# Router in the output projection, a first gather for one pair, and the last pair's down projection by column halves

## The chip, the cores and the metric

One core of one Trainium2 chip runs the whole program in one launch. The metric is the device time of an execution in microseconds. The median of three runs of the kernel before is 4315.71 us (4311.06 to 4321.27).

## What is computed

Two transformer blocks over 512 latent tokens (and 256 context tokens) of width 1024 in float32, and a third one at whose end stands a mixture of experts. Only the end of that third block is touched: the output projection `w_o` with its residual and norm, and the mixture, in which each expert picks its own 64 tokens of the 512:

```
x_mid = x + mod_x[2] * (merged @ w_o)
h2 = modulate(rms(x_mid, norm2_g), mod_x[3], mod_x[4])
affinity = softmax(h2 @ router_w)                     # 512 x 16 experts
gate, idx = top_k(affinity.T, 64)                     # 64 tokens for each expert
xe = h2[idx]                                          # 16 x 64 x 1024
hid = silu(xe @ w_gate[e]) * (xe @ w_up[e])           # 1024 x 1408 each
ye = (hid @ w_down[e]) * gate                         # 1408 x 1024
out = x_mid + mod_x[5] * scatter_add(ye, idx)
```

The three weight tensors of the 16 experts are 277 MB, and each is read once.

## The kernel before, in words

A kernel is a row of phases. Each ends with a clearing of its semaphores by SP and a barrier of all engines (`phase`). Within a phase each engine runs its own instruction list and waits on semaphores; all loads and stores are issued by SP, in program order, on one hardware queue.

**Output projection** (`closing`, tag `wo`). 512 tokens are four tiles of 128. For each of two column blocks and four tiles, eight matmuls accumulate (L488), PSUM bank `u % 6`. Behind the last block's tiles VectorE forms `x`, ScalarE its sum of squares, VectorE the normed tile `y` (`x_hat`, L579). TensorE turns it, two tiles behind (`behind = 2`, `turn`, L451, eight transposes into banks 6 and 7), and ScalarE and VectorE take four blocks each with the modulation (L516, L586) into `hT`. SP loads the router's weights once block 0 is done (`then`, L72).

**Router** (`route`). SP loads three constants (L4357 to L4359), and then the nine first ring pieces. TensorE makes the logits, four tiles x eight matmuls with 16 columns (L4369). VectorE and ScalarE make the softmax (L4403 to L4408). TensorE turns the affinities to 16 rows of 512, VectorE finds the 64 largest of each row in eight rounds of `max` and `match_replace`, TensorE turns the mask back and ranks it, and `picks` (L4434) writes the one-hot matrix `pick` (token x slot) for the first four experts, 256 slots.

**Experts** (`experts`). SP first loads three vectors (`experts_cols`, L4480 to L4482) and the last gate (L4483, 512 KB). TensorE gathers the first four experts' tokens: for each of eight blocks of features k, four matmuls over the token tiles (`gather`, L4501), stationary `x_hat[:, tile, k::8]`, moving `pick` with 256 columns. A float32 matmul is two weight loads and two matmul instructions in the trace, a transpose one of each. ScalarE applies the modulation (`take`, L4619), which needs `mul` (L4638), made from the three vectors; TensorE's first expert matmul waits for all eight blocks. VectorE picks for the other 12 experts once the gate has landed.

The experts go in eight pairs. The two of a pair have 64 slots each and stand side by side in the array's columns. For each step j of eight, 12 matmuls (24 instructions, L4572) use the step's two pieces (gate and up rows j of either expert, 2 x 1408 floats of each partition, 1.44 MB) and accumulate in six banks; side 0 and side 1 write different banks at a time (`(m % 2) ^ side`). Then `hid` is formed, turned (L4586), and the down projection (L4605) goes over 11 row blocks of 128 in pieces of two rows (1.05 MB), into banks 6 and 7, again crosswise. VectorE multiplies by the gate (L4688), and eight matmuls of the scatter (L4514) bring the result back to tokens, with an addition each (L4648). Between the steps stand `fillers`, in a fixed order: in pair 0 four blocks of the next gather and then eight turns of the gated picks (L4509), two fillers after each of the first steps (`max(10 - 2 * j, 0)`); in later pairs gathers for pairs ahead and the scatter of the pair before. After the last pair come its gating, eight scatters, eight additions and four stores of 512 KB (L4494).

The ring has room for nine gate-and-up pieces. `expert_places` lays 224 pieces into it; a piece that would run over the end starts at 0. Each piece waits in SP for the release of the last piece that lay in its place. Pieces 0 to 8 wait for nothing. Piece 9 waits for piece 0, and so on to 16 (the first down piece) for 7; 17 waits for 8, 18 for 9, and from there several small ones go into the place of one large one. A step's two pieces are released by its last matmuls, before the fillers behind it.

## Time and profile before

| what | us |
|---|---|
| median of the runs | 4315.71 |
| the profiled execution's own time | 4313.52 |
| its span | 4311.7 |
| output projection ends, route starts | 3599.1, 3599.9 |
| experts phase starts | 3635.2 |
| first expert matmul | 3654.0 |
| last down matmul ends | 4298.7 |

Over the span TensorE is busy 92%, VectorE 37%, ScalarE 20%, GpSimd 16%. The table of slices shows the last 16% of the span with DMA at 400 to 422 GB/s and TensorE at 8 to 9 tenths; in the two slices before, DMA moves 40 and 145 GB/s. The share of busy time is a mean over stages of different kinds, so it must be read together with the slices: in one stage the matmuls may set the pace, in another the loads.

### The profile page before, as it was taken

Reading aid. Unit: us, or ns where it says so; the run is one execution under the profiler, and the core shown is the slowest. Engines: PE = TensorE matmul, PEld = TensorE weight load, DVE = VectorE, ACT = ScalarE, POOL = GpSimd, SP = SyncE. Lnnn points to the kernel's source line nnn. Section 1 sums busy time; section 2 is a strip of 40 time slices with the busy share of each in tenths; the row PEclk is TensorE's granted clock in tenths of the full one; section 3 lists DMA queues with packets and bytes.
Section 4 is the critical chain, followed back from the end, with each engine's and each line's share of the span. In section 5 each row is a group of like instructions: output and inputs, shape, how many; then the busy total and the mean of one; then the engine's idle time right before and its main releaser. Section 6 shows DMA issues by size and latency. Waiting matters only on the chain. (4 is left out here: it accounts for less than half of the span.)

```text
span 4311.7 us, 50124 instructions
## 1 busy us (share of the span) xinstructions
PE 3985.8 (92%) x20395; PEld 2380.8 (55%) x20395; DVE 1590.6 (37%) x2962; ACT 850.7 (20%) x1656; POOL 690.9 (16%) x513
## 2 busy tenths in 40 slices
PE   7997889999989999899988999989998897999988
PEld 4665445554446766588546666664554445433433
DVE  2346442224734464433464454530123323111111
ACT  3224320000123332200013233320123201000000
POOL 0003212223411111122333232310002200000000
PEclk9998999999999999999998999999999997999999
DMA  4117511113431111353341010104200313999998
GB/s 171 40 37 256 191 40 59 59 59 132 167 98 44 40 45 59 111 207 133 128 122 46 23 28 21 37 21 150 62 1 1 156 40 145 401 421 422 422 421 368
DMA packets 317260, 580.04 MB, mean 135 GB/s; under 512 B 55933, under 2 KB 186333, under 8 KB 316393
## 3 DMA queue, kind: packets, MB, share of 16 engines
q1 hardware_dynamic: 317032, 576.84, 36.4%
q8 instruction: 164, 2.69, 0.2%
q14 instruction: 64, 0.52, 0.0%
HBM read 566.15 MB, written 10.63 MB: 134 GB/s over the span
## 5 line engine op out<-in xcount | busy, mean ns | idle before, releaser
L3018 PE MATMUL dn_ps<-room,dn_w 128*128 128x512 f32 (+1 forms) x616 | 229.7, 526 | 5.2 <-DVE dn_qx L3556 3.5
L776 PE MATMUL ffn_up_ps<-room,ffn_up_w 128*128 128x384 f32 (+1 forms) x704 | 209.0, 441 | 12.4 <-DMA ffn_up_w<-in_ffn_w_gate 12.4
L776 PE MATMUL ffn_up_ps<-ffn_up_t,room 128*128 128x384 f32 (+1 forms) x704 | 205.9, 436 | 1.0 <-DVE room L856 1.0
L776 PE MATMUL ffn_up_ps<-room 128*128 128x384 f32 (+1 forms) x704 | 203.9, 432 | 0.0
L4572 PE MATMUL experts_ps<-experts_ring,experts_xs 128*64 128x512 f32 (+1 forms) x768 | 165.5, 582 | 28.0 <-DMA experts_ring<-in_w_up 28.0
L776 PEld LDWEIGHTS ffn_up_ps<-room,ffn_up_w 128*128 128x128 f32 x704 | 135.3, 194 | 71.6 <-DMA ffn_up_w<-in_ffn_w_gate 13.2
L4572 PE MATMUL experts_ps<-experts_ring,room 128*64 128x512 f32 (+1 forms) x768 | 162.7, 576 | 8.0 <-DMA experts_ring<-in_w_up 7.3
L3018 PEld LDWEIGHTS dn_ps<-room,dn_w 128*128 128x128 f32 x616 | 117.0, 195 | 96.0 <-issue 82.5
L2415 PE MATMUL hgrn_ps<-room,hgrn_w 128*128 128x512 f32 x372 | 168.7, 593 | 0.7 <-DMA hgrn_w<-in_odd_w_in 0.7
L776 PEld LDWEIGHTS ffn_up_ps<-ffn_up_t,room 128*128 128x128 f32 x704 | 134.7, 192 | 58.1 <-DVE room L856 2.3
L1051 PE MATMUL ffn_down_ps<-ffn_down_w_sums,ffn_down_hid_sums 128*128 128x512 f32 x330 | 163.2, 604 | 2.2 <-DVE ffn_down_w_sums L1139 2.2
L776 PEld LDWEIGHTS ffn_up_ps<-room 128*128 128x128 f32 x704 | 133.8, 190 | 55.7
L4605 PE MATMUL experts_ps<-experts_ring,experts_hidT 128*64 128x512 f32 x704 | 154.6, 594 | 10.5 <-issue 5.6
L4648 DVE TENSOR_TENSOR x_sb<-x_sb,experts_ps 128x512 f32<-128x512 f32 x64 | 44.0, 687 | 302.9 <-PE experts_ps L4514 302.9
L863 DVE TENSOR_TENSOR room<-ffn_up_ps,room 128x384 f32<-128x384 f32 (+1 forms) x154 | 73.3, 488 | 222.2 <-PE ffn_up_ps L776 222.2
L2412 PE MATMUL hgrn_ps<-hgrn_w,room 128*128 128x384 f32 (+1 forms) x480 | 144.0, 451 | 0.0
L4572 PEld LDWEIGHTS experts_ps<-experts_ring,experts_xs 128*64 128x64 f32 x768 | 59.4, 141 | 135.1 <-issue 132.1
L488 PE MATMUL out_ps<-out_w,room 128*128 128x512 f32 x296 | 130.4, 599 | 0.8 <-ACT room L530 0.8
L1051 PE MATMUL ffn_down_ps<-ffn_down_w,ffn_hid 128*128 128x512 f32 x220 | 116.5, 612 | 15.3 <-DMA ffn_down_w<-in_ffn_w_down 14.5
L834 POOL TENSOR_TENSOR room<-ffn_up_w 128x512 f32<-128x512 f32 x44 | 56.7, 1289 | 439.6 <-PE ffn_up_ps L776 233.0
L188 PE MATMUL in_ps<-in_w,room 128*128 128x512 f32 (+1 forms) x296 | 119.9, 565 | 0.6 <-DMA in_w<-in_w_in 0.6
L1139 DVE TENSOR_TENSOR ffn_down_w_sums<-ffn_down_w,ffn_down_w_sums 128x512 f32<-128x512 f32 x55 | 81.9, 1490 | 96.9 <-POOL ffn_down_w_sums L1114 96.9
(628 smaller groups left out, 6891.9 us busy)
## 6 DMA issues: line engine op xcount, KB each, us to landing
experts_ring<-in_w_gate SPq DMA_DIRECT2D x128, 704.0 KB, 15.5
experts_ring<-in_w_up SPq DMA_DIRECT2D x128, 704.0 KB, 17.8
experts_ring<-in_w_down SPq DMA_DIRECT2D x160, 512.0 KB, 14.3
ffn_down_w<-in_ffn_w_down SPq DMA_DIRECT2D x55, 1024.0 KB, 4.9
att_wm<-in_mod_w SPq DMA_DIRECT2D x20, 2048.0 KB, 9.2
ffn_up_wm<-in_ada_w SPq DMA_DIRECT2D x12, 2048.0 KB, 12.5
ffn_up_w<-in_ffn_w_up SPq DMA_DIRECT2D x22, 1024.0 KB, 7.7
ffn_up_w<-in_ffn_w_gate SPq DMA_DIRECT2D x20, 1024.0 KB, 5.5
```

Of the source, the lines that this page charges most:

```text
L188: mm = nc.tensor.matmul(ps[:, u % 8, 0:wd], xT[:, k, t * P:(t + 1) * P], ahead.tile[:, k, 0:wd] if j == 0 and k < n_ahead else wt[:, j % r ...
L488: mm = nc.tensor.matmul(ps[:, u % BANKS, 0:wd], xT[:, k, t * P:(t + 1) * P], wt[:, j % ring, k, 0:wd], start=k == 0, stop=k == kt - 1)
L776: mm = nc.tensor.matmul(result(n, p), lhs[:, k, :], rhs[:, k, :], start=k == 0, stop=k == half - 1)
L834: nc.gpsimd.tensor_tensor(s[:, 0, :, :], quarter(n, 1, lo), quarter(n, 1, hi), ALU.add).then_inc(S["s1_done"], 1)
L863: nc.vector.tensor_tensor(kept(n, to), result(n, p), kept(n, q), ALU.add).then_inc(done, 1)
L1051: mm = nc.tensor.matmul(result(p, prod), lhs, rhs, start=j == 0, stop=j == STEPS - 1)
L1139: nc.vector.tensor_tensor(t[:, 1, :], hi[:, right], t[:, 0, :], ALU.subtract).then_inc(S["t2_done"], 1)
L2412: mm = nc.tensor.matmul(ps[:, bank, 0:b - a], hT[:, k, t * P:(t + 1) * P], wt[:, s, k, 0:b - a], start=k == 0, stop=k == KD - 1)
L2415: mm = nc.tensor.matmul(ps[:, bank, :], weights(j, k)[:, piece * P:(piece + 1) * P], hT[:, k, CTX:], start=k == 0, stop=k == KD - 1)
L3018: mm = nc.tensor.matmul(out, ahead.tile[:, k, :] if k < by_ahead else wt[:, h % 2, piece, k, :], hT[:, k, tok], start=k == 0, stop=k == KD ...
L4572: mm = nc.tensor.matmul(ps[out_rows, 3 * n + c, 0:b - a], xs_now[:, j, at:at + SLOTS], ring[:, w_at + a:w_at + b], start=j == 0, stop=j == ...
L4605: mm = nc.tensor.matmul(ps[out_rows, 6 + half, :], hidT[:, f, out_rows], ring[:, w_at:w_at + 512], start=f == 0, stop=f == FT - 1)
```

## The change

The `Router` object holds the router's weights, the constants (identity, upper triangle, ones, slot numbers) and room for the softmax. Its five loads are issued where that of the router's weights was. The logits of a tile are made in `closing`, one turn behind, in bank 2. The exponentials and the reciprocal of their sum are made at the end of the same phase. `route` begins with their product. The first picks are for two experts, 128 slots, and the first gather as well; the other half of that group of four experts ("second") is eight fillers ahead of the others in pair 0, which are now up to three after a step. The picks in `experts` are for 14 experts. The last pair's down projection goes over all 11 row blocks for columns 0 to 511, and then for columns 512 to 1023, in pieces of four, four and three row blocks; each half has its own gating, four scatters and four stores.

```diff
+class Router:
+
+    def __init__(self, w, tables, sem, srcs, first):
+        E = EXPERTS
+        lat = TILES - CTX_TILES
+        self.tile = first[:, 0:KD * E].rearrange("p (k e) -> p k e", k=KD)
+        at = KD * E
+        self.exps = first[:, at:at + lat * E].rearrange("p (m e) -> p m e", m=lat)
+        at += lat * E
+        self.red = first[:, at:at + 3 * lat].rearrange("p (j m) -> p j m", j=3)
+        self.pairs, self.at = [(self.tile, w)], {}
+        at = 0
+        for name, src, width in srcs:
+            self.at[name] = tables[:, at:at + width]
+            self.pairs.append((self.at[name], src))
+            at += width
+        self.sem, self.loads = sem, len(self.pairs)
+
+    def load(self, sp):
+        for dst, src in self.pairs:
+            sp.dma_start(dst, src).then_inc(self.sem, 16)
...
+            LOGITS = 2
+
+            def logits(n):
+
+                if n == 0:
+                    pe.wait_ge(router.sem, 16 * router.loads)
+                    pe.wait_ge(S["yg_done"], LOGITS + 1)
+                pe.wait_ge(S["taken_a"], n + 1)
+                pe.wait_ge(S["taken_d"], n + 1)
+                for k in range(KD):
+                    mm = nc.tensor.matmul(ps[:, LOGITS, n * EXPERTS:(n + 1) * EXPERTS], hT[:, k, tiles[n] * P:(tiles[n] + 1) * P], router.tile[:, k, :], start=k == 0, stop=k == KD - 1)
+                mm.then_inc(S["logits"], 1)
...
                         turn(tiles[i - behind])
-            for t in tiles[-behind:]:
-                turn(t)
+                        if router and i > behind:
+                            logits(i - behind - 1)
+            for n in range(n_tiles - behind, n_tiles):
+                turn(tiles[n])
+                if router:
+                    logits(n - 1)
+            if router:
+                logits(n_tiles - 1)
...
+            if router:
+                act.wait_ge(S["shifted"], 1)
+                nc.scalar.activation(router.exps, router.exps, ACT.Exp).then_inc(S["exp_done"], 1)
...
+            if router:
+                shape = [P, n_tiles, EXPERTS]
+                logits = ps[:, 2, 0:n_tiles * EXPERTS].rearrange("p (m e) -> p m e", m=n_tiles)
+                dve.wait_ge(S["logits"], n_tiles)
+                nc.vector.tensor_reduce(router.red[:, 0, :], logits, AX.X, ALU.max).then_inc(S["top_done"], 1)
+                dve.wait_ge(S["top_done"], 1)
+                nc.vector.tensor_tensor(router.exps, logits, router.red[:, 0, :].unsqueeze(2).broadcast_to(shape), ALU.subtract).then_inc(S["shifted"], 1)
+                dve.wait_ge(S["exp_done"], 1)
+                nc.vector.tensor_reduce(router.red[:, 1, :], router.exps, AX.X, ALU.add).then_inc(S["exp_sum"], 1)
+                dve.wait_ge(S["exp_sum"], 1)
+                nc.vector.reciprocal(router.red[:, 2, :], router.red[:, 1, :]).then_inc(S["inverted"], 1)
+                dve.wait_ge(S["inverted"], 1)
...
-            sp.dma_start(cst[:, :, :], I["tables"][:, 0:2, :]).then_inc(S["const_in"], 16)
-            sp.dma_start(ones, I["ones"]).then_inc(S["const_in"], 16)
-            sp.dma_start(slot_iota[:, :], I["slot_numbers"]).then_inc(S["const_in"], 16)
...
-            pe.wait_ge(ahead.sem, 16)
-            for m in range(tiles):
-                for k in range(KD):
-                    mm = nc.tensor.matmul(ps[:, 0, m * E:(m + 1) * E], hT[:, k, (CTX_TILES + m) * P:(CTX_TILES + m + 1) * P], w[:, k, :],
-                                          start=k == 0, stop=k == KD - 1)
-            mm.then_inc(S["logits"], 1)
-            pe.wait_ge(S["const_in"], 48)
             pe.wait_ge(S["aff_done"], 1)
...
-                picks(nc, pick, slot, slot_iota, m, 0, GROUP)
-
...
-        ahead = [("gather", pair // 2 + 1, 4 * (pair % 2) + i) for i in range(4)] if pair < pairs - 2 else []
+        ahead = [("second", 0, k) for k in range(KD)] if pair == 0 else []
+        ahead += [("gather", pair // 2 + 1, 4 * (pair % 2) + i) for i in range(4)] if pair < pairs - 2 else []
...
+    xs_whole = {("first", 0): slice(0, P), ("second", 0): slice(P, 2 * P)}
+    LAST = pairs - 1
+    SCATTERED = 2 * tiles * LAST
+    last_banks = (0, 1, 2, 3, 4, 5, 6, 0)
...
-
-                sp.wait_ge(S["scatter_out"], (pairs - 1) * 2 * tiles + 2 * m + 2)
-                sp.dma_start(out_v[:, m, :], x[:, CTX_TILES + m, :]).then_inc(S["stored"], 16)
-            sp.wait_ge(S["stored"], 16 * tiles)
+            for half in range(2):
+                cols_of = slice(half * 512, (half + 1) * 512)
+                for m in range(tiles):
+                    sp.wait_ge(S["scatter_out"], SCATTERED + half * tiles + m + 1)
+                    sp.dma_start(out_v[:, m, cols_of], x[:, CTX_TILES + m, cols_of]).then_inc(S["stored"], 16)
+            sp.wait_ge(S["stored"], 16 * 2 * tiles)
...
+            def gather(what, k, group, bank):
+                part = xs_whole.get((what, group), slice(0, 2 * P))
+                first, end = 2 * group * P + part.start, 2 * group * P + part.stop
                 for m in range(tiles):
-                    mm = nc.tensor.matmul(ps[:, bank, 0:2 * P], x_hat[:, CTX_TILES + m, k::KD], pick[:, m, 2 * group * P:(2 * group + 2) * P],
-                                          start=m == 0, stop=m == tiles - 1)
+                    mm = nc.tensor.matmul(ps[:, bank, 0:end - first], x_hat[:, CTX_TILES + m, k::KD], pick[:, m, first:end], start=m == 0, stop=m == tiles - 1)
...
+            def scatter_last(n):
+                half, m = divmod(n, tiles)
+                if n == len(last_banks) - 1:
+                    pe.wait_ge(S["scatter_out"], SCATTERED + 1)
+                nc.tensor.matmul(ps[:, last_banks[n], :], pick_gateT[:, LAST, m * P:(m + 1) * P], ye[:, LAST % 2, half * 512:(half + 1) * 512],
+                                 start=True, stop=True).then_inc(S["scatter_mm"], 1)
+
             for k in range(KD):
-                gather(k, 0, k)
+                gather("first", k, 0, k)
...
-                pe.wait_ge(S["gather_out"], KD * (pair // 2 + 1))
+                pe.wait_ge(S["gather_out"], KD * (pair // 2 + 2) if pair else KD)
...
-                    while len(fill) > (max(AFTER_UP, 12 - 2 * (j + 1) if j < 4 else 7 - j) if pair else max(10 - 2 * j, 0)):
+                    while len(fill) > (max(AFTER_UP, 12 - 2 * (j + 1) if j < 4 else 7 - j) if pair else max(17 - 3 * j, 0)):
...
+                    half, a, b = down_parts(pair)[j - KD]
+                    if half is not None:
+                        for f in range(a, b):
+                            for n, (first, end) in enumerate(t_jobs):
+                                if half == 0 and f == first:
+                                    pe.wait_ge(S["hid_turned"], len(cuts) * pair + n + 1)
+                            for side in range(2):
+                                out_rows = slice(SLOTS * side, SLOTS * (side + 1))
+                                w_at = places[pair * pieces + 2 * j + side][0] + (f - a) * 512
+                                mm = nc.tensor.matmul(ps[out_rows, 6 + half, :], hidT[:, f, out_rows], ring[:, w_at:w_at + 512], start=f == 0, stop=f == FT - 1)
+                        if b == FT:
+                            mm.then_inc(S["half_mm"], 1)
+                        if half and b < FT:
+                            if a == 0:
+                                pe.wait_ge(S["half_out"], 1)
+                            for n in range(2):
+                                scatter_last((0 if a == 0 else 2) + n)
+                        continue
...
+            pe.wait_ge(S["half_out"], 2)
+            for n in range(tiles, 2 * tiles):
+                scatter_last(n)
...
+            def take(what, k, group, bank, count):
+                part = xs_whole.get((what, group), slice(0, 2 * P))
                 act.wait_ge(S["gather_mm"], count)
-                nc.scalar.activation(xs[group % 2][:, k, :], ps[:, bank, 0:2 * P], ACT.Identity, scale=mul[:, k:k + 1], bias=cols[:, 2, k:k + 1]).then_inc(S["gather_out"], 1)
+                nc.scalar.activation(xs[group % 2][:, k, part], ps[:, bank, 0:part.stop - part.start], ACT.Identity, scale=mul[:, k:k + 1], bias=cols[:, 2, k:k + 1]).then_inc(S["gather_out"], 1)
...
-            for i in range(2 * tiles):
-                add(2 * tiles * (pairs - 1) + i, i, i)
+            dve.wait_ge(S["scatter_mm"], 2 * tiles * (LAST - 1))
+            dve.wait_ge(S["scatter_out"], SCATTERED)
+            for half in range(2):
+                cols_of = slice(half * 512, (half + 1) * 512)
+                dve.wait_ge(S["half_mm"], half + 1)
+                nc.vector.tensor_tensor(ye[:, LAST % 2, cols_of], ps[:, 6 + half, :], gate[:, cols_of], ALU.mult).then_inc(S["half_out"], 1)
+                for m in range(tiles):
+                    n = half * tiles + m
+                    dst = x[:, CTX_TILES + m, cols_of]
+                    dve.wait_ge(S["scatter_mm"], SCATTERED + n + 1)
+                    nc.vector.tensor_tensor(dst, dst, ps[:, last_banks[n], :], ALU.add).then_inc(S["scatter_out"], 1)
 
...
+def down_parts(pair):
+
+    FT = EXPERT_FF // P
+    if pair < EXPERTS // 2 - 1:
+        return [(None, a, b) for a, b in expert_rows()]
+    return [(half, a, min(a + 4, FT)) for half in range(2) for a in range(0, FT, 4)]
...
+            if half is not None:
+                to = ring[:, at:at + (b - a) * 512].rearrange("p (f d) -> p f d", d=512)
+                for f0, f1 in ((a, a + 2), (a + 2, b)):
+                    sp.dma_start(to[:, f0 - a:f1 - a, :], src[:, f0:f1, half * 512:(half + 1) * 512]).then_inc(landed, 16)
+                return
```

## Rows read from the trace of the kernel before

**Rows 1.** windows: busy us (count) of PE, PEld, DVE, ACT, POOL; clock, DMA, GB/s

```profile
3640.00:3660.00 20.00, 19.34 (x82) 15.56 (x82) 5.83 (x6) 3.94 (x7) 0.00 (x0) 0.98 0.01 2
4100.00:4290.00 190.00, 165.78 (x739) 64.26 (x737) 26.21 (x39) 5.05 (x9) 0.00 (x0) 0.98 1.02 421
```

**Rows 2.** the chain that ended last, its end; start, us, what

```profile
4293.28 5.38 PE experts_ps L4605 x24
4298.69 1.23 DVE room L4688
4299.97 7.15 PE experts_ps L4514 x16
```

**Rows 3.** timeline across the two phases; start, us, engine, line, what

```profile
3597.76 1.37 DVE L586 TENSOR_SCALAR room<-wo_ps,wo_mul,wo_cols 128x128 f32<-128x128 f32 x4 [1.26 <-PE wo_ps L451]
3599.96 13.81 PE L4369 MATMUL route_ps<-first,room 128*128 128x16 f32 x64 [2.25 <-PEq L47]
3601.25 1.26 SPq L4734 DMA_DIRECT2D experts_ring<-in_w_gate  x1
3613.88 0.22 DVE L4403 TENSOR_REDUCE route_red<-route_ps 128x4 f32<-128x64 f32 x1 [14.76 <-PE route_ps L4369]
3615.15 0.23 DVE L4408 TENSOR_TENSOR gates<-gates,route_red 128x64 f32<-128x64 f32 x1
```

**Rows 4.** one-microsecond windows, and a timeline row of the last turn

```profile
3593.00:3594.00 1.00, 0.00 (x0) 0.00 (x0) 0.15 (x1) 0.81 (x2) 0.00 (x0) 0.60 0.00 0
3641.00:3642.00 1.00, 1.00 (x6) 1.00 (x5) 1.00 (x2) 0.15 (x1) 0.00 (x0) 1.00 0.00 0
3595.77 1.94 PE L451 MATMUL wo_ps<-cst,room 128*128 128x128 f32 x8 [3.32 <-ACT room L516]
```

**Rows 5.** timeline and chain at the start of the experts phase

```profile
3635.26 18.08 PE L4501 MATMUL experts_ps<-pick,room 128*128 128x256 f32 x64 [2.75 <-PEq L47]
3637.72 0.17 DVE L4638 SCALAR_TENSOR_TENSOR experts_mul<-experts_cols 128x8 f32<-128x8 f32 x1 [3.19 <-DMA experts_cols<-mod]
3653.99 4.95 PE experts_ps L4572 x24
```

**Rows 6.** landing of small loads (`experts_cols`, then `wo_cols`), and a window

```profile
DMA to landing us min/median/max: 1.6/1.6/1.7
DMA to landing us min/median/max: 4.8/5.7/6.3
3634.00:3635.00 1.00, 0.00 (x0) 0.00 (x0) 0.53 (x2) 0.00 (x0) 0.00 (x0) 0.50 0.48 197
```

**Rows 7.** weight loads (min/median/max ns), a timeline row, a window

```profile
L4501 PEld LDWEIGHTS experts_ps<-pick,room x14: 313/342/342, 3635.2 to 3640.5; 128*128 128x128 f32 x14
L4501 PEld LDWEIGHTS experts_ps<-pick,room x50: 315/337/338, 3641.0 to 3652.7; 128*128 128x128 f32 x50
L776 PEld LDWEIGHTS ffn_up_ps<-ffn_up_t,ffn_up_w x8: 190/190/190, 1833.5 to 1835.0; 128*128 128x128 f32 x8
1560.04 1.05 PE L2435 MATMUL hgrn_ps<-hgrn_qmix,hgrn_kmix 128*128 128x128 f32 x8
3641.00:3652.00 11.00, 11.00 (x48) 11.00 (x47) 4.87 (x5) 3.36 (x6) 0.00 (x0) 1.00 0.01 1
```

**Rows 8.** fillers of pair 0 in the chain, and a window

```profile
3658.93 4.14 PE experts_ps L4501 x16
3676.96 1.02 PE experts_ps L4509 x8
3668.00:3670.00 2.00, 2.00 (x8) 2.00 (x9) 0.00 (x0) 0.00 (x0) 0.00 (x0) 1.00 0.50 90
```

**Rows 9.** a timeline row of the first stage, and windows

```profile
22.70 3.68 PE L290 MATMUL n_ps<-n_w,conditions 128*2 128x128 f32 x128
4295.00:4296.00 1.00, 1.00 (x8) 0.47 (x6) 0.00 (x0) 0.00 (x0) 0.00 (x0) 1.00 0.05 18
3540.00:3544.00 4.00, 4.00 (x11) 1.75 (x10) 0.24 (x2) 0.00 (x0) 0.00 (x0) 1.00 1.05 397
```

More of the change, by code:

```diff
@@ L4334, in quarter_tables, with route @@
     return {name: np.ascontiguousarray(t.astype(np.float32)) for name, t in tables.items()}
-def route(nc, tag, hT, I, cst, ones, slot_iota, slot, pick, aff, work, load, places, ahead):
+def route(nc, tag, slot, pick, aff, work, load, places, router):
     tiles = TILES - CTX_TILES
@@ L4345, in sb @@
             return stack.enter_context(nc.sbuf_tensor(f"{tag}_{name}", [P, *shape], F32))
-        w = ahead.tile
-        red = sb("red", 4, tiles)
+        ident, upto, ones, slot_iota = (router.at[name] for name in ("ident", "upto", "ones", "slots"))
         top = sb("top", 8)
@@ L4535, in filler @@
                         pe.wait_ge(*done[-2])
-                    if what == "gather":
-                        if of == 1 and i == 0:
+                    if what in ("second", "gather"):
+                        if what == "second" and i == 0:
                             pe.wait_ge(S["picked"], tiles)
-                        if i % 4 == 0:
+                        if what == "gather" and i % 4 == 0:
                             pe.wait_ge(S["up_mm"], len(cuts) * (2 * of - 2))
-                        gather(i, of, bank)
+                        gather(what, i, of, bank)
                         gathered += 1
@@ L4623, in _ @@
             for k in range(KD):
-                take(k, 0, k, k + 1)
+                take("first", k, 0, k, k + 1)
             for pair in range(pairs):
                 for i, (what, of, k) in enumerate(fillers(pair)):
-                    if what == "gather":
-                        take(k, of, 6 + i % 2, n_gather[pair] + i + 1)
+                    if what in ("second", "gather"):
+                        take(what, k, of, 6 + i % 2, n_gather[pair] + i + 1)
                 if pair:
@@ L4707, in expert_places @@
 def expert_places():
-    sizes = [size for pair in range(EXPERTS // 2) for size in [2 * EXPERT_FF] * (2 * KD) + [(b - a) * D for a, b in expert_rows() for side in range(2)]]
+    sizes = [size for pair in range(EXPERTS // 2) for size in [2 * EXPERT_FF] * (2 * KD) + [(b - a) * (D if half is None else D // 2) for half, a, b in down_parts(pair) for side in range(2)]]
     places, at = [], 0
@@ L4772, in second_block, with mixture @@
     branches(nc, "mix2", hT, I["w_out_a_2"][0], I["w_out_b_2"][0], delta_out, proj, I["dn_norm_g_2"][0], mix, spare, ident, mix2, wo.load)
-    closing(nc, "wo", hT, KD, wo_jobs, x, mix, hT, ident, (mod, 2, None), (I["norm2_g_2"][0], mod, 3, 4), CTX_TILES, ahead=wo, then=router.load)
+    closing(nc, "wo", hT, KD, wo_jobs, x, mix, hT, ident, (mod, 2, None), (I["norm2_g_2"][0], mod, 3, 4), CTX_TILES, ahead=wo, then=router.load, router=router)
     return router
-def mixture(nc, I, out, x, room, hT, mix, cst, ident, mod, first, router):
+def mixture(nc, I, out, x, room, mix, mod, first, router):
     n_slots = EXPERTS * SLOTS
@@ L4823, in program @@
             router = second_block(nc, I, x, hT, mix, cst, cst[:, IDENT, :], mod2, first, (even_in, odd_in), dn)
[L4824 to L4826 removed]
+        mixture(nc, I, out, x, room, mix, mod2, first, router)
 INPUTS = (
```

65 lines of the change are left out of this document (23 added, 42 removed).

## The prediction

> **What bounds the kernel now.** I read the engine shares, the slices, the chain that ended last, and then the stretches of the mixture of experts in ever shorter windows. TensorE is busy 92% of the span, but over the last 650 us this is the wrong figure: from 4100 to 4290 us the DMA engines are at 1.02 and move 421 GB/s while TensorE is busy 166 of 190 us [rows 1]. The expert weights are 16 x 3 x 1024 x 1408 x 4 B = 277 MB, so this stage ends when the last piece has landed, plus a tail. Its start is not bound by DMA: between 3640 and 3660 the share is 0.01 [rows 1]. The ring holds nine gate-and-up pieces of 1.44 MB; they are in by 3634.5, and the tenth can be loaded only when TensorE has read the first. So the end of the kernel moves with three things: the time of the first release, the time the queue stands still after it, and the tail behind the last landing. The tail is 24 down matmuls from 4293.28, the gating (1.23 us), 16 scatter instructions (7.15 us), adds and stores [rows 2].
>
> **Router.** Before, the tiles are normed and turned by 3599.13, the route phase starts at 3599.96, its 64 logit instructions take 13.81 us (0.216 each), and maximum, exponential, sum and reciprocal last from 3613.88 to 3615.12 [rows 3]. The clock was granted at 0.60 in the microsecond from 3593, after TensorE had begun to stand between the turns, and the last turn ran at 1.2 GHz, 1.94 us for eight instructions; back at 2.4 GHz it would be 1.05 as in the like row [rows 4, 7]. In the new order logits of tiles 0 and 1 (16 instructions, 1.7 us each at 0.108) fill those gaps, and I take the clock to stay up. The last turn then begins at 3595.77 and ends at 3596.85, tile 2's logits at 3598.6, tile 3's at 3600.3, softmax (1.24) at 3601.65, and with the 0.8 us of the hand-over route starts at 3602.45, 2.5 later than now. It begins with the product that now starts at 3615.15 [rows 3], so everything after is 12.7 us earlier; four picks over 128 in place of 256 elements give some 0.5 more, and the experts phase starts near 3622.0 for 3635.2. Bounds: 1.7 us later for 2.5 if only tile 3's logits show, 6.5 if the clock falls all the same. The three constant loads ahead of the weights go (1.34 us of issue), so the first weight DMA moves from 3601.25 to 3602.4, and the ring is full at about 3635.1 for 3634.5 [rows 3, 6].
>
> **First gather.** The two columns' loads of `mul` and the shift are issued at the start of the experts phase. Now they land in 1.6 us, on an empty queue. In the new kernel they are issued at 3622 behind 5.5 MB of ring loads. The nearest rows are the same small loads in the output projection, behind 2 MB: 4.8 to 6.3 us [rows 6]. So I let them land when the ring is full, near 3636.3; `mul` is ready at 3636.5 (3637.72 now), and ScalarE needs 8 x 0.4 for the gathered blocks: the first expert matmul starts near 3639.8, not 3633. By the Trainium skill (DMA: Bandwidth & Descriptors, "Queues, rings and completion order") each DMA engine consumes one queue's descriptors in ring order; the landing times above agree. If they are not held back, 2 us are gained here.
>
> How long is a gather of 128 slots? The stationary operand is `x_hat[:, tile, k::8]`, read at a stride of 32 bytes. Its weight loads take 342 ns at the half clock and 337 at the full one, where the ones read in line take 190, and in the full-clock stretch the loads are busy 11.00 of 11.00 us [rows 7]. So the gather is bound by its weight loads, at some 0.24 us per instruction, whatever is streamed. Halving the slots halves the streamed columns and leaves all 64 weight loads. The first gather falls from 18.08 to about 64 x 0.24 = 15.4 us and ends at 3637.4, just before the blocks are taken. The first release is then at 3639.8 + 4.9 = 3644.7, 14.2 earlier than 3658.9 [rows 5].
>
> By the Trainium skill (SBUF — State Buffer, the note on cachelines in "Door 1: The DMA port swizzle") a read that goes to a new 16-byte line with each element pays a penalty; the 337 against 190 ns agree. But the Trainium skill (TensorE: Matmul & The Clock Gate, "LDWEIGHTS") gives columns/1.2 ns for a weight load, an estimate of 107 ns for 128 columns and no word of the stride: by that the narrow gather would be the first rival below.
>
> **Second gather.** Its 64 instructions are new work inside pair 0, on the path, because TensorE releases the pieces. Eight narrow gathers are put at 3, 3 and 2 behind the first three steps, one wide gather and three more follow, then the turns at three a step. A step's matmuls are 4.88 us (from the 4.95 with its tail), a wide gather 2.07 (4.14 for two), two turns 1.02 [rows 5, 8]. A narrow gather is between 1.05 (the like row with weights in line, eight instructions [rows 7]) and 2.07; I take 1.95 = 8 x 0.24 and a little. Two gate-and-up pieces need 6.83 us of DMA. The queue stands for the difference:
> - steps 1 and 2: 3 x 1.95 + 4.88 = 10.7, stands 3.9 each;
> - step 3: 2 x 1.95 + 2.07 + 4.88 = 10.85, stands 4.0;
> - step 4: 3 x 2.07 + 4.88 = 11.1, for pieces of 1.44 and 1.05 MB (5.9 us), stands 5.2;
> - step 5: 1.5 + 4.88 = 6.4, for two of 1.05 MB (5.0 us), stands 1.4.
>
> That is 18.4 us. Now only two steps are long, 9.02 - 6.83 = 2.2 each, 4.4 in all, seen as the 90 GB/s after 3668 [rows 8]. So 14.0 of the 14.2 us gained are given back before pair 0 is over: -0.2 at the last landing. From step 6 on TensorE is faster than DMA, as now; pair 1's two long steps (4.4) are covered by the slack of the down part (19 against 27 us). The new picks of 14 experts (4.2 us on VectorE behind the gate's landing, near 3643) are ready before the first narrow gather at 3644.7. A delay up to 1 us there would count.
>
> **Last pair by halves.** Same bytes, in runs of 2 KB for 4 KB. The nearest row with 2 KB runs is the `w_o` load, 397 GB/s against 421 [rows 9, 1]: 11.5 MB would cost 0 to 1.6 us more; I take 1.0. Now everything has landed at 4295.1 [rows 9] and the span ends at 4311.7, 16.6 later. New tail from the last landing: the step before it (16 matmuls 3.6, two scatters 1.8) is still running until +1.9, then the last three blocks (12 instructions, 2.7) to +4.4; gating of one half with its hand-over 0.75; four scatters 8 x 0.43 + 0.17 = 3.6; last add 0.86; store and end 3.6 (3.9 now, from the last add to 4311.7). Together 13.2: -3.4. Bounds: -5.1 if nothing of the earlier step is left over, -2 if it ends 1.4 us later, as loads that land unevenly over the last microseconds, as now, would make it.
>
> **Sum.** -0.2 + 1.0 - 3.4 = -2.6 us on the profiled execution (4313.5 for a span of 4311.7). The median of the runs is 4315.7, 2.2 above it, so I forecast 4313. No change is what a measurement tells within 0.2%, 8.6 us.
>
> **Rivals.**
> - The narrow gather runs at the rate of weights read in line, 1.05 us. For: the turns read the same stride, and even at the half clock eight took 1.94 us [rows 4], less than 0.24 apiece before the last one's tail. Against: the gather's own loads of 337 ns, busy all the time. Then TensorE idles from 3633 to 3639.8, the first step loses 2.8 us to the half clock, which held from 3635.3 to 3641 after the idle of now [rows 4, 5] (release 3647.5, -11.4), and the stops are 1.2, 1.2, 2.2, 5.2, 1.5 = 11.3, +6.9. With +1.0 and -3.4: -6.9, 4309. If the small loads aren't held back either: gathers done at 3633, release near 3639 with the clock up, about -16, 4300.
> - Slower: the halves don't overlap. Now the two experts' matmuls of a pair write different banks at any moment; in the halves both write one bank, in two groups of partitions. If these went one after the other, a half's 44 instructions would take 18.9 us, not 9.5; half 1 would not be done with 13.6 us of loads but some 16 us later than in the sum: 4329. It decides once the pitch of L4605's successor is above 0.31 us (13.6/44). Against: in the first stage four column groups write one bank, 128 instructions in 3.68 us, 29 ns each for 128 columns [rows 9], which is only possible side by side.
> - The half clock holds through the closing, or the gather's gaps are larger: +4 on the sum's start, 4317.
>
> **How the numbers follow.** My forecast 0.48; narrow gather fast 0.20; that and the small loads free 0.08; slower start 0.13; halves one after another 0.06; effects not seen here 0.05. The forecast's own range is 4308 to 4319. To hold 8 in 10 it is 4303 to 4321. Faster by over 0.2% (below 4307): the free loads 0.08, a third of the fast gather 0.07, and 0.03 for what I don't see, 0.18. Slower by over 0.2% (above 4324): the halves 0.06, 0.04 of the slower start, 0.02 unseen, 0.12. Within: 0.70.
>
> **What would show it.** The new route phase starts near 3602.5 and has no 64-instruction group. `experts_mul` at 3636.5, not 3625, shows the small loads held. A first gather of 15 us, and three narrow gathers in 5.9 us between the matmuls of the first step and of the second, show the weight-load bound; 3.2 us would refute it. DMA windows of pair 0 should stand still for some 18 us in five places. The last pair's down instructions should keep their 0.22 us pitch, and the tail behind the last landing be 13 us. I am wrong if the last landing moves by more than 4 us.

## The result

| | kernel before | kernel changed |
|---|---|---|
| median of 16 runs each, us | 4317.77 | 4324.82 |
| lowest to highest, us | 4311.06 to 4324.38 | 4316.66 to 4332.88 |
| ratio to before, 95% interval | | 1.0018 (1.001 to 1.0026) |
| span of the profiled execution, us | 4311.7 | 4331.1 |
| first matmul of the last output projection, us | 3531.5 | 3545.2 |
| from there to the end (the "stretch"), us | 780.2 | 785.9 |

The forecast was 4313 (4303 to 4321), 2.6 us below before. The kernel is some 7 us slower, 0.18% by the ratio, and 4324.82 lies outside the range.

Of the 19.4 us between the two spans, 13.7 had arisen before the first touched instruction ran. The changed kernel's profiled execution, at 4332.88, is the slowest of its 16. In stretches of unchanged code its clock was low where it had been full: two windows of it, then the same of before (columns as in [rows 1], absolute times).

```profile
440.00:445.00 5.00, 5.00 (x78) 3.60 (x75) 2.85 (x6) 2.79 (x6) 1.58 (x2) 0.71 0.13 47
476.00:482.00 6.00, 4.87 (x24) 3.24 (x28) 2.01 (x6) 3.50 (x8) 2.63 (x1) 0.72 0.56 213
```

```profile
440.00:445.00 5.00, 4.23 (x69) 3.36 (x70) 4.38 (x9) 3.20 (x7) 2.17 (x2) 1.00 0.85 287
476.00:482.00 6.00, 5.76 (x107) 4.40 (x97) 4.50 (x12) 4.33 (x10) 3.36 (x2) 1.00 0.66 213
```

Over all traces of this case the start of the stretch scatters from 3531.2 to 3545.2 us. So traces are compared here by the stretch and by times counted from its start, and kernels by their medians too. The same kernel profiled twice gave stretches of 770.8 and 770.0.

**Closing and route**, timeline of the kernel after, TensorE and then VectorE (it answers [rows 3, 4]):

```profile
3602.76 1.05 PE L475 MATMUL wo_ps<-cst,room 128*128 128x128 f32 x8
3603.64 1.86 PE L497 MATMUL wo_ps<-first,room 128*128 128x16 f32 x16
3605.35 1.12 PE L475 MATMUL wo_ps<-cst,room 128*128 128x128 f32 x8
3606.31 2.74 PE L497 MATMUL wo_ps<-first,room 128*128 128x16 f32 x16
3609.49 1.94 PE L475 MATMUL wo_ps<-cst,room 128*128 128x128 f32 x8 [0.45 <-ACT room L559]
3611.23 6.85 PE L497 MATMUL wo_ps<-first,room 128*128 128x16 f32 x32
3618.11 0.22 DVE L713 TENSOR_REDUCE first<-wo_ps 128x4 f32<-128x64 f32 x1 [5.27 <-PE wo_ps L497]
```

and the clock in windows (the last figures of a row are granted clock, DMA share, GB/s):

```profile
3606.00:3607.00 1.00, 1.00 (x12) 1.00 (x11) 0.34 (x1) 0.62 (x1) 0.00 (x0) 1.00 0.00 0
3607.00:3608.00 1.00, 1.00 (x7) 1.00 (x7) 0.17 (x2) 0.78 (x4) 0.00 (x0) 0.53 0.00 0
3612.00:3616.00 4.00, 4.00 (x21) 4.00 (x20) 0.84 (x3) 1.41 (x2) 0.00 (x0) 0.50 0.00 0
```

The logits do fill the gaps between the turns: TensorE is busy 1.00 us in each microsecond from 3596 to 3609. All the same the clock goes from 2.4 to 1.2 GHz inside that busy stretch (0.53 from 3607), and the last 32 logit instructions take 6.85 us where the first 16 took 1.86.

**First gather and the small loads** (it answers [rows 5 to 7]): timeline; then the landing of the later of the two `mod` loads; then weight loads of a narrow gather at full clock; then two windows around the stand in front of the first expert step.

```profile
3639.84 15.53 PE L4539 MATMUL experts_ps<-pick,room 128*128 128x128 f32 x64 [2.16 <-PEq L47]
3655.00 0.17 DVE L4701 SCALAR_TENSOR_TENSOR experts_mul<-experts_cols 128x8 f32<-128x8 f32 x1 [15.82 <-DMA experts_cols<-mod]
3655.21 2.91 ACT L4682 ACTIVATE room<-experts_ps,experts_cols,experts_mul 128x128 f32<-128x128 f32 x8 [36.32 <-DVE experts_mul L4701]
3658.16 6.64 PE L4616 MATMUL experts_ps<-experts_ring,room 128*64 128x512 f32 x24 [2.79 <-ACT room L4682]
```

```profile
DMA to landing us min/median/max: 14.3/14.3/14.3
```

```profile
L4539 PEld LDWEIGHTS experts_ps<-pick,room x24: 312/335/336, 3664.7 to 3670.2; 128*128 128x128 f32 x24
```

```profile
3656.00:3657.00 1.00, 0.00 (x0) 0.00 (x0) 1.00 (x2) 1.00 (x5) 0.00 (x0) 1.00 0.00 0
3659.00:3660.00 1.00, 1.00 (x6) 0.38 (x4) 1.00 (x2) 0.00 (x0) 0.00 (x0) 0.50 0.00 0
```

The gather of half as many slots takes 15.53 us, 15.4 forecast; that its strided weight loads of 335 ns set its pace is shown by e5 below. The two columns were issued at 3640.2 and 3640.7 behind the ring and landed when it was full, so `mul` came at 3655.0 and TensorE stood 2.79 us. Then the clock fell to 0.50, which the forecast's sum did not have: the first expert step takes 6.64 us where the later ones take 4.95.

**Pair 0**, timeline of TensorE, and windows in which the queue stands (they answer [rows 8]):

```profile
3664.74 5.98 PE L4539 MATMUL experts_ps<-pick,room 128*128 128x128 f32 x24
3670.65 4.95 PE L4616 MATMUL experts_ps<-experts_ring,room 128*64 128x512 f32 x24
3675.52 6.01 PE L4539 MATMUL experts_ps<-pick,room 128*128 128x128 f32 x24
3697.26 6.13 PE L4539 MATMUL experts_ps<-pick,room 128*128 128x256 f32 x24
```

```profile
3672.00:3674.00 2.00, 2.00 (x12) 0.71 (x10) 0.00 (x0) 0.00 (x0) 0.00 (x0) 1.00 0.67 279
3674.00:3676.00 2.00, 2.00 (x12) 0.91 (x9) 0.00 (x0) 0.00 (x0) 0.00 (x0) 1.00 0.00 0
3684.00:3686.00 2.00, 2.00 (x14) 0.72 (x10) 0.00 (x0) 0.00 (x0) 0.00 (x0) 1.00 0.17 70
3696.00:3698.00 2.00, 2.00 (x13) 1.04 (x10) 0.00 (x0) 0.00 (x0) 0.00 (x0) 1.00 0.00 0
3706.00:3708.00 2.00, 2.00 (x14) 0.67 (x10) 0.00 (x0) 0.00 (x0) 0.00 (x0) 1.00 0.00 0
3716.00:3718.00 2.00, 1.65 (x10) 0.76 (x10) 2.00 (x3) 0.00 (x0) 0.00 (x0) 1.00 0.67 225
```

How long the queue stands in all is read from one window of 76 us behind the first release, here of the kernel before and then of the kernel after:

```profile
3659.00:3735.00 76.00, 75.70 (x371) 37.17 (x371) 12.24 (x17) 5.79 (x9) 0.00 (x0) 1.00 0.96 382
```

```profile
3664.80:3740.80 76.00, 75.01 (x360) 43.76 (x361) 10.93 (x16) 8.89 (x16) 0.00 (x0) 1.00 0.79 298
```

At 421 GB/s all the time nothing would be lost: the loss is 76 x (421 - 382)/421 = 7.0 us before and 22.2 us after. The difference is 15.2 us, 14.0 forecast.

**Tail** (it answers [rows 2]), timeline and a window:

```profile
4314.30 3.65 PE L4647 MATMUL experts_ps<-experts_ring,experts_hidT 128*64 128x512 f32 x16
4319.80 2.80 PE L4647 MATMUL experts_ps<-experts_ring,experts_hidT 128*64 128x512 f32 x12
4323.39 3.70 PE L4558 MATMUL experts_ps<-room 128*128 128x512 f32 x8 [0.80 <-DVE room L4760]
```

```profile
4318.00:4319.00 1.00, 1.00 (x3) 0.52 (x4) 0.00 (x0) 0.00 (x0) 0.00 (x0) 1.00 0.10 31
```

Sixteen instructions in 3.65 us, 0.23 each, where those of the output projection, 128 columns wide, take 0.43 (96 in 41.36 us): the halves' two groups run side by side. The last bytes land near 4318.2, and the span ends 12.9 us later (13.2 forecast, 16.6 before).

### The profile page after: what moved, and what is told of

The parts are those of the page before. It is cut to its first block and busy times, and to the rows that moved or that the text cites. A ratio compares the mean times of both kernels' runs of the same rounds, so it can differ in the third digit from the quotient of the medians.

```text
span 4331.1 us, 50262 instructions
## 1 busy us (share of the span) xinstructions
PE 4007.9 (93%) x20459; PEld 2397.8 (55%) x20459; DVE 1590.6 (37%) x2963; ACT 853.5 (20%) x1664; POOL 691.4 (16%) x513
## 5 line engine op out<-in xcount | busy, mean ns | idle before, releaser
L834 PEld LDWEIGHTS ffn_up_ps<-room,ffn_up_w 128*128 128x128 f32 x704 | 135.3, 194 | 71.6 <-DMA ffn_up_w<-in_ffn_w_gate 13.2
L4616 PE MATMUL experts_ps<-experts_ring,room 128*64 128x512 f32 (+1 forms) x768 | 164.4, 580 | 10.9 <-DMA experts_ring<-in_w_up 8.1
L4666 PE MATMUL experts_ps<-experts_ring,experts_hidT 128*64 128x512 f32 x616 | 135.1, 594 | 7.0 <-issue 4.0
L1109 PE MATMUL ffn_down_ps<-ffn_down_w,ffn_hid 128*128 128x512 f32 x220 | 116.5, 612 | 15.1 <-DMA ffn_down_w<-in_ffn_w_down 14.4
L4616 PEld LDWEIGHTS experts_ps<-experts_ring,room 128*64 128x64 f32 x768 | 55.1, 141 | 115.2 <-issue 111.6
## 6 DMA issues: line engine op xcount, KB each, us to landing
experts_ring<-in_w_down SPq DMA_DIRECT2D x160, 512.0 KB, 14.2
```

The source lines that it names most:

```text
L834: mm = nc.tensor.matmul(result(n, p), lhs[:, k, :], rhs[:, k, :], start=k == 0, stop=k == half - 1)
L1109: mm = nc.tensor.matmul(result(p, prod), lhs, rhs, start=j == 0, stop=j == STEPS - 1)
L4616: mm = nc.tensor.matmul(ps[out_rows, 3 * n + c, 0:b - a], xs_now[:, j, at:at + SLOTS], ring[:, w_at + a:w_at + b], start=j == 0, stop=j == ...
L4666: mm = nc.tensor.matmul(ps[out_rows, 6 + half, :], hidT[:, f, out_rows], ring[:, w_at:w_at + 512], start=f == 0, stop=f == FT - 1)
```

## The experiments

Each is the changed kernel with one or more edits. Times are in us; the first three columns and the stretch count from the first matmul of the last output projection. "Release" is the end of the first expert step, "loss" the queue's in the 76 us behind it (good to 0.2 us: it moves by that much when the window is shifted by 0.1). Both medians of a row are of the same comparison on one chip.

| kernel | first ring load | first expert matmul | release | stretch | loss | median, before's median | ratio (95%) |
|---|---|---|---|---|---|---|---|
| before | 69.8 | 122.5 | 127.5 | 780.2 | 7.0 | | |
| after | 75.2 | 113.0 | 119.6 | 785.9 | 22.2 | 4324.8, 4317.8 | 1.0018 (1.0010 to 1.0026) |
| e1 logits only | 75.1 | 113.9 | 118.9 | 773.2 | 7.6 | 4308.6, 4316.5 | 0.9982 (0.9974 to 0.9991) |
| e2 logits, halves | 75.2 | 113.9 | 118.9 | 770.8 | 7.0 | 4306.0, 4316.5 | 0.9972 (0.9962 to 0.9983) |
| e12 as e2, again | 75.1 | 113.9 | 118.8 | 770.0 | 7.0 | 4308.3, 4314.5 | 0.9985 (0.9976 to 0.9994) |
| e11 as e2, wide logits | 71.7 | 110.8 | 115.7 | 766.8 | 6.5 | 4301.9, 4314.5 | 0.9974 (0.9963 to 0.9985) |
| e3 wide logits | 71.6 | 109.4 | 115.9 | 782.7 | 22.0 | 4319.4, 4316.5 | 1.0011 (1.0001 to 1.0020) |
| e4 early vectors | 75.1 | 110.7 | 115.7 | 783.0 | 22.4 | 4319.4, 4316.5 | 1.0007 (0.9998 to 1.0016) |
| e5 features in line | 75.6 | 113.8 | 121.6 | 780.6 | 12.6 | 4317.2, 4316.5 | 1.0006 (0.9997 to 1.0015) |
| e6 in line, early vectors | 75.5 | 104.7 | 109.7 | 775.5 | 20.8 | 4314.2, 4316.5 | 0.9993 (0.9984 to 1.0001) |
| e9 as e6, picks first | 75.6 | 104.9 | 109.9 | 767.5 | 12.8 | 4303.9, 4314.3 | 0.9976 (0.9967 to 0.9984) |
| e7 as e6, wide gather | 75.6 | 112.1 | 117.1 | 767.5 | 5.6 | 4303.0, 4316.5 | 0.9968 (0.9958 to 0.9978) |
| e8 as e7, wide logits | 72.1 | 108.6 | 113.6 | 763.6 | 5.8 | 4303.8, 4316.5 | 0.9970 (0.9959 to 0.9982) |
| e10 as e9, wide logits | 72.0 | 101.5 | 106.4 | 764.0 | 12.8 | 4302.8, 4314.3 | 0.9968 (0.9956 to 0.9979) |

### Undoing the narrow gather, and the halves (e1, e2)

```diff
-PAIR = 2
+PAIR = 4
-        ahead = [("second", 0, k) for k in range(KD)] if pair == 0 else []
-        ahead += [("gather", pair // 2 + 1, 4 * (pair % 2) + i) for i in range(4)] if pair < pairs - 2 else []
+        ahead = [("gather", pair // 2 + 1, 4 * (pair % 2) + i) for i in range(4)] if pair < pairs - 2 else []
-                    while len(fill) > (... if pair else max(17 - 3 * j, 0)):
+                    while len(fill) > (... if pair else max(10 - 2 * j, 0)):
```

e1 has in addition the last pair's down projection of before.

> Times are read from the first matmul of the output projection to the end of the span: 780.2 us in the profile of before, 785.9 after. Theory A (the second gather costs the gain: its weight loads are as long as a wide gather's, and they stand in pair 0, where TensorE sets the releases): with only the router's part of the change kept, the first expert matmul starts 8 us earlier than before, the queue stands still only 4.4 us after the first release, and the stretch is 772. Theory B (the gain is lost elsewhere, because the ring's first loads start 5.4 us later than before and DMA bounds the stage): 785.

> The change without its narrow gathers. Theory A: as the router alone, with 2 us more of loads (2 KB runs and an uneven end) and 3.7 us less of tail: 770. Theory C (the halves cost more than they bring, by their loads): above 772, 3 us or more longer than the router alone.

Measured: 773.2 and 770.8, for 772 and 770 expected (e1's loss of 7.6 for 4.4 was too low an expectation: before itself loses 7.0). The part with the logits alone is faster than before; the narrow gather turns it round: from e2 to the whole change the stretch grows by 15.1 us. It brings nothing even at its start, since the first release comes at 119.6 with it and at 118.9 without: `mul` waits for the queue until 109.8 with it and until 109.9 without, and with the shorter gather TensorE stands and loses its clock. The halves bring 2.4 us net, the forecast's +1.0 - 3.4. That the two agree so well is partly luck: 0.6 us of it lies in pair 0, which the halves don't touch, and with e12, the same kernel again, it is 3.2.

### Logits 128 columns wide (e3)

```diff
-  mm = nc.tensor.matmul(ps[:, LOGITS, n * EXPERTS:(n + 1) * EXPERTS], hT[...], router.tile[:, k, :], ...)
+  mm = nc.tensor.matmul(ps[:, LOGITS, n * P:(n + 1) * P], hT[...], router.wide[:, k * EXPERTS:k * EXPERTS + P], ...)
```

> The logits' matmuls of the changed kernel stream 128 columns in place of 16; the other 112 are left unused in the same bank. Theory A (the clock falls because the narrow logits stream hardly any columns, and this is what makes route start 4.3 us later than I forecast): the clock stays at 2.4 GHz to the last logits, each tile's 16 instructions take some 2 us, route starts 18 to 21 us after the first turn of the last block in place of 25.4, and the stretch is 781 to 782. Theory B (it falls with the end of the projection's long matmuls, whatever small ones follow): 25.4 and 786.

Measured: same instructions, eight times the columns, and less time. Timeline and a window of e3:

```profile
3592.52 1.95 PE L498 MATMUL wo_ps<-first,room 128*128 128x128 f32 x16
3599.69 3.74 PE L498 MATMUL wo_ps<-first,room 128*128 128x128 f32 x32
```

```profile
3600.00:3602.00 2.00, 2.00 (x20) 2.00 (x19) 1.26 (x4) 1.87 (x3) 0.00 (x0) 1.00 0.00 0
```

The granted clock is 1.00 in every window of the closing up to the end of the logits, although TensorE stood 1.22 us before the last turn (0.45 in the changed kernel), the 32 last logit instructions take 3.74 us for 6.85, and the first ring load comes 3.6 us earlier. The same is seen in every other kernel here: 6.84 or 6.85 us in all nine with 16 columns, 3.74 in all four with 128. The stretch is 3.2 us shorter, 782.7 for the 781 to 782 expected. So what the forecast lacked here was not cover: the engine was covered at least as well in the changed kernel, and only the columns differ.

### The three vectors loaded early (e4)

```diff
+        for n, src in enumerate(vectors):
+            self.pairs.append((cols[:, n, :], src))
-            sp.dma_start(cols[:, 0, :], column(gain)).then_inc(S["cols_in"], 16)
...
-            dve.wait_ge(S["cols_in"], 48)
```

> The changed kernel with the three small vectors loaded beside the router's weights, ahead of the ring. Theory A (they wait for the queue to drain): mul is ready at once, the first expert matmul follows the narrow gather by 0.7 us in place of 2.8, at the full clock; first release 4 us earlier, stretch 782. Theory B (the wait is covered by something else): no more than 1 us.

Measured: 783.0, for 782 expected. `mul` is ready at the phase's start and the first step runs at once after the gather, at full clock:

```profile
3627.20 15.53 PE L4540 MATMUL experts_ps<-pick,room 128*128 128x128 f32 x64 [2.16 <-PEq L47]
3643.28 4.95 PE L4617 MATMUL experts_ps<-experts_ring,room 128*64 128x512 f32 x24 [0.55 <-ACT room L4683]
```

Held vectors and half clock together cost 119.63 - 115.66 = 4.0 us at the first release and 2.9 in the stretch.

### The gather's features in line (e5, e6, e9)

`x_hat` is written with the 128 features of a block side by side, so that the gather's stationary operand has no stride. e6 adds the early vectors. e9 moves a wait too.

```diff
-  x_hat[:, CTX_TILES + m, k::KD]
+  x_hat[:, CTX_TILES + m, k * P:(k + 1) * P]
```

> The changed kernel with x_hat stored block by block, so that the gather's stationary operand is 128 neighbouring columns in place of every eighth. Stretch as before, from the first matmul of the output projection: 785.9 in the changed kernel. Theory A (the weight loads at a stride set the pitch): weight loads of 190 ns at the full clock, three narrow gathers in 3.2 to 3.6 us in place of 5.9, a wide one 1.75; the stops in pair 0 fall from 18 to 10 us; the first expert matmul still waits for the small vectors, now at the half clock, 1 us worse. Stretch 778 to 779. Theory B (the pace of the narrow gathers is ScalarE's, which takes each block out of two banks in turn): 5.9 stays, 786.

> Both edits, weights side by side and the vectors early. Theory A: the narrow first gather takes about 10 us and nothing stands behind it: first expert matmul 105 us after the projection's first matmul in place of 113.0, stretch 768 to 769; the router with the halves alone had 770.8. Theory B (the two overlap): 775.

Measured in e5, timeline and weight loads inside pair 0:

```profile
3626.25 9.35 PE L4539 MATMUL experts_ps<-pick,room 128*128 128x128 f32 x64 [2.16 <-PEq L47]
3645.01 7.83 PE L4616 MATMUL experts_ps<-experts_ring,room 128*64 128x512 f32 x24 [9.41 <-ACT room L4682]
3652.76 2.94 PE L4539 MATMUL experts_ps<-pick,room 128*128 128x128 f32 x24
```

```profile
L4539 PEld LDWEIGHTS experts_ps<-pick,room x24: 186/192/192, 3652.8 to 3655.3; 128*128 128x128 f32 x24
```

and a window inside e5's first gather:

```profile
3628.00:3635.00 7.00, 7.00 (x55) 7.00 (x54) 0.00 (x0) 0.00 (x0) 0.00 (x0) 0.83 1.02 423
```

Three narrow gathers fall from 5.98 to 2.94 us, a weight load from 335 to 192 ns, the queue's loss from 22.2 to 12.6 us. The stride is the whole of the narrow gather's slowness; ScalarE, theory B, was not its limit. It is this run that shows it, and not the busy share that the forecast argued from: in e5 the weight loads are busy 7.00 of 7.00 us too, at a pace twice as fast, and 64 loads of 335 ns one after another would be 21.4 us, not 15.5, so they overlap. The Trainium skill says of strided reads in general that they pay a penalty (SBUF — State Buffer, the note on cachelines in "Door 1: The DMA port swizzle"), and the 335 against 192 ns agree. But e5's stretch, 780.6, is longer than the 778 to 779 expected: the shorter gather only lets TensorE stand 9.4 us for the held vectors, and the first step takes 7.83 us.

e6 was expected at 768 to 769 and came at 775.5. Its expectation missed a wait, which the timeline shows:

```profile
3649.53 4.10 DVE L4467 TENSOR_TENSOR pick<-x_sb,slot 128x896 f32<-128x896 f32 x4 [15.95 <-DMA first<-mod]
3653.69 4.82 PE L4540 MATMUL experts_ps<-pick,room 128*128 128x128 f32 x24 [5.64 <-DVE pick L4467]
```

The picks of the other 14 experts stand behind a wait for the last gate, which lies behind the ring in the queue. In the changed kernel they came in time because the first expert step, which waited for the same queue, was as late. In e9 the wait is moved behind the picks, which don't use the gate:

```diff
-            dve.wait_ge(S["gate_in"], 16)
             ...
             for m in range(tiles):
                 picks(nc, pick, slot, slot_iota, m, PAIR, EXPERTS).then_inc(S["picked"], 1)
+            dve.wait_ge(S["gate_in"], 16)
```

> The changed kernel with the features of the gather's tokens in line, the three vectors loaded early, and VectorE's picks for the other 14 experts ahead of its wait for the last gate, not behind it. Theory A: of the kernel with the first two edits alone, the 5.6 us that TensorE stood before its first narrow gather, and the 1.9 us that the half clock then cost it, are due to this wait alone: both go, the three narrow gathers take 2.94 us and the stretch is 768 us (767 to 769) for 775.5. Rival B: the narrow gather is slow inside the pair for another reason (ScalarE, PSUM banks): the stretch stays at 774 or more.

Measured: 767.5, as expected (768), and

```profile
3647.36 2.94 PE L4540 MATMUL experts_ps<-pick,room 128*128 128x128 f32 x24
3650.23 4.94 PE L4617 MATMUL experts_ps<-experts_ring,room 128*64 128x512 f32 x24
```

### Wide gather with all of it; wide logits with all of it (e7, e8, e10)

> Router and halves with the wide first gather, weights side by side and the vectors early. The first gather falls from 18.1 to about 16.7 us, a wide gather between the steps from 2.07 to 1.75, so the two stops in pair 0 from 4.4 to 3.1: 768, as good as the narrow gather when nothing is strided. Rival: with the streamed 256 columns as the limit nothing is gained, 771.

> The same with the logits streaming 128 columns. If gains add, 3.5 us less: 764 to 765, and 15 us less than before. Rival (the 3.5 us are taken by the queue, which then fills the ring earlier but stands longer): 768.

> The same with the logits made 128 columns wide. Theory A: the clock stays up in the closing as in the kernel with a wide gather (763.6 us), and the stretch is 3.6 us under the one without wide logits, 764 to 765 us. By that the narrow gather, at its best, is worth 0 to 1 us against the wide one: the first release comes 7.4 us earlier, and 6.5 to 7.5 us are given back in pair 0. Rival B: the narrow gather keeps what it gains at the first release, 760 us or less.

Measured: stretches of 767.5, 763.6 and 764.0, within 0.5 us of what was expected. The narrow gather at its best (e9, e10) and the wide one (e7, e8) are equal: the release comes 7.1 to 7.2 us earlier, and the queue's loss grows by 7.0 to 7.2 us (12.8 for 5.6 and 5.8). Where the weights set the pace no longer, the second gather is still work put on the path before the release of pieces; it can't bring a gain while TensorE, not the queue, is late in pair 0.

### Do wide logits show in the medians (e11, e12)?

The wide logits had shortened three stretches by 3.2 to 3.9 us, but the medians of e8 and e7 differ by +0.9 us, those of e10 and e9 by -1.1.

> The logits in the output projection and the halves of the last pair, with the first gather again for four experts, and the logits 128 columns wide. Theory A: the clock stays up in the closing, the first ring load comes 3.5 us earlier and with it everything behind: the stretch is 767.2 us for the 770.8 of the same kernel with 16-column logits, and its median is 3 to 4 us under that kernel's in the same comparison. Rival B: the start is earlier but the median isn't, since the wider matmuls cost time in a place that one profiled execution does not show: less than 1 us between the two medians.

> The logits in the output projection and the halves of the last pair, with the first gather again for four experts and the logits 16 columns wide, beside the one with wide logits on the same chip. Theory A: stretch 770.8 us as measured before, median 3 to 4 us above the one with wide logits. Rival B: medians within 1 us of each other.

Measured: 766.8 and 770.0, medians 4301.9 and 4308.3, so 6.4 us apart for the 3 to 4 of theory A and the less than 1 of rival B. Four pairs of kernels differ by the wide logits alone. Their medians differ by -4.2 (e3 and the change, each against its own before: 2.8 - 7.05), +0.9, -1.1 and -6.4 us. The mean is -2.7, near the 3.5 of the stretches; single pairs scatter by some 4 us about it. That wide logits help the median is likely, not shown beyond the scatter.

The lowest medians are those of e11 (4301.9), e10, e7, e8 and e9 (4303.9): each 10 to 14 us below its own before, so some 17 to 21 below the change, and not told apart among themselves. All beat both kernels.

## Why the prediction was wrong

Its sum against the traces, each as a shift against before, in us:

| step | forecast | measured |
|---|---|---|
| first ring load | +1.2 | +5.4 |
| first gather begins | -13.2 | -9.1 |
| `mul` ready, behind the ring | -1.2 | +3.6 |
| first expert matmul | -14.2 | -9.5 |
| first release | -14.2 | -7.9 |
| queue stands longer in pair 0 | +14.0 | +15.2 |
| 2 KB runs and what is unassigned | +1.0 | +2.1 |
| tail | -3.4 | -3.7 |
| sum | -2.6 | +5.7 |

The sum adds the release and the three rows below it; the rows above lead to the release. The measured last landing moved by +9.4 = -7.9 + 15.2 + 2.1; the 2.1 is what is left over; the last pair's loads moved at 406 and 408 GB/s (4290 to 4310), which for 11.5 MB makes the forecast 1.0 of it. It was forecast at +0.8, and by more than 4 us the forecast was to count as wrong by its own words.

- **The step that failed is "I take the clock to stay up" in the closing.** It put the route 2.5 us later than before and named 6.5 as the bound "if the clock falls all the same". It fell. The last turn begins at 64.3 in before, the changed kernel and e3 alike; the product that opens the route follows it by 6.7 us in the forecast, by 10.9 in the changed kernel and by 7.4 in e3, whose clock stays up. The first expert matmul waits for `mul`, `mul` for the ring and the ring for the route, so these 4.3 us came through to it. The forecast took busy time for activity: filled gaps were to keep the clock. The windows show TensorE busy and the clock at 0.53; with 128 columns in the same instructions it stays at 1.00 (e3). By the Trainium skill (TensorE: Matmul & The Clock Gate, "What's actually happening") a monitor sets the clock by how busy the array has been; a busy share in the profile is, by these windows, no measure of that.

  The trace of before held the warning. Its 64 logit instructions, 16 columns wide and back to back, ran at half clock to their end, 13.8 us later:

```profile
3602.00:3606.00 4.00, 4.00 (x21) 4.00 (x20) 0.00 (x0) 0.00 (x0) 0.00 (x0) 0.50 0.75 234
3606.00:3610.00 4.00, 4.00 (x21) 4.00 (x20) 0.00 (x0) 0.00 (x0) 0.00 (x0) 0.50 1.02 424
```

  The forecast read 0.216 us apiece from them and halved it.
- **A second step was left out: the half clock behind the stand for the vectors.** The forecast had TensorE stand 2.4 us, from 3637.4 to 3639.8, and then run the first step in 4.9 us. It stood 2.8 and took 6.64 for 4.95, which makes +1.6 at the first release. The rival with the fast gather had counted just this loss, for a longer stand. e4 removes both and gives a step of 4.95.
- **The rest held.** Weight loads set the narrow gather's pace (15.53 for 15.4 us, 5.98 for 5.85 inside the pair), and e5 shows the stride as the cause; the rival of the fast gather was wrong. The small loads were held. The halves run side by side; the tail came out within 0.3, so the slower rival of the forecast did not occur.
- **The stops agree within 1.2 us, in part by luck.** Their difference was forecast at 14.0 and came at 15.2, but both terms were too low: 22.2 for 18.4 after, 7.0 for 4.4 before. Step by step the queue of the changed kernel loses 3.9, 3.9, 4.0 and 5.0 us, as forecast, then 2.0 and 1.9 behind steps 5 and 6 (299 and 306 GB/s over 6.9 us each), of which one was counted, at 1.4; 1.4 more are lost behind them. Before has a third stop of 1.7 us (298 GB/s from 3677 to 3683) and 1.0 behind it, neither in the forecast.
- **The rival that came true** is the last, "half clock through the closing, or larger gaps", at 0.13 and 4317. It too was too low, since it held only the first of the slips: 4.3 (closing) + 0.4 (rest of the way to the first matmul) + 1.6 (its half clock) + 1.2 (stops) + 1.1 (runs and unassigned) - 0.3 (tail) = 8.3, the distance from -2.6 to +5.7. The sum was a difference of two large terms, -14 and +14; every slip in them had the same sign, and the range of 18 us had no room for that. The 1.1 is not assigned to a cause. With the clock kept up alone (e3) the stretch would still be 2.5 us longer than before.
- Of the 11.8 us between 4313 and 4324.82, 2.1 are no slip of a step: the forecast started from the median of three runs of before, 4315.71, and 16 runs give 4317.77. The changed kernel's excess in the medians, 7.05, and in the stretch, 5.7, agree within the scatter; the 13.7 us between the profiled executions ahead of the stretch is scatter of untouched code. What makes the clock fall there in some executions was not tried.

## What to carry to other kernels

When work is moved so that a resource starts earlier, ask who delivers the next release after that: here half of the gather went from ahead of the first release to between the releases; it cost 15.1 us and brought the first release no earlier (119.6 with it, 118.9 without). Read what sets the pace of an instruction (here the strided weight load) before its width is cut: half the columns saved 2.6 of 18.1 us (1.8 of the 17.3 that the wide one takes in e2). A small load that the next step needs is issued ahead of a long run of large ones on the same queue, and a wait stands only before what uses its data.

## What the runs showed of the hardware

- 16-column float32 matmuls with their weight loads, back to back, neither kept TensorE at 2.4 GHz nor brought it there: in the changed kernel the granted clock fell from 1.00 to 0.50 with the engine busy 1.00 of each us, and in before it stayed at 0.50 for 13.8 busy us. At 128 columns, same count, it stayed at 1.00 and the 32 instructions took 3.74 instead of 6.85 us.
- A 128x128 float32 weight load with its elements 32 bytes apart took 335 ns, one in line 192 ns; the pitch of the narrow gather's instructions fell from 0.25 (5.98/24) to 0.12 us (2.94/24).
- After TensorE had stood 2.8 us, the clock fell to 0.50 and the next step took 6.64 for 4.95 us; after 9.4 us (e5), 7.83.
- Two groups of 64 columns that write one bank ran side by side: 16 instructions of 512 columns in 3.65 us, 0.23 each, for 0.43 at full width.
- A load of 4 KB issued behind some 5.6 MB of the ring (412 GB/s over the 13.7 us from 3640.7) landed after 14.3 us, and after 1.6 on the empty queue [rows 6].
